# A projection tile moved into the index-score stage of a hybrid decoder block, with three PSUM pairs for the scores

## The reference, cut to what matters

```
h    = rmsnorm(x) * (1 + sc1) + sh1
proj = h @ w_in                      # cq, k, v, ki, wi, rq, rf, ri, rg, gates
qi   = rmsnorm(cq) @ w_uq_idx        # index queries, 8 heads of 64
q    = rmsnorm(cq) @ w_uq            # attention queries
score[t, s] = sum over heads of wi[t, head] * relu(qi[t, head] . ki[s])
f    = lb + (1 - lb) * sigmoid(rf)   # forget gate of the recurrence, head by head
qq   = silu(rq)                      # its query
```

## Time and profile before

| | |
|---|---|
| median of 3 runs | 1731.77 us (1730.85 to 1731.93) |
| the profiled execution | 1735.35 us |
| its span, first to last instruction | 1733.5 us |
| mean granted PE clock | 0.969 of full speed |
| PE busy | 1594.8 us, 92% |
| DVE busy | 1045.3 us, 60% |
| ACT busy | 713.5 us, 41% |
| POOL busy | 493.1 us, 28% |

### The profile page before, as it was taken

The page is one execution under the profiler, slowest core; times in us unless marked ns, Lnnn a source line. Parts: engine busy times, 40 slices in busy tenths (PEclk is TensorE's granted clock), DMA queues, the critical chain, the costliest instruction groups (busy, mean ns, idle before and its releaser), DMA issues.

```text
span 1733.5 us, 21047 instructions
## 1 busy us (share of the span) xinstructions
PE 1594.8 (92%) x7451; PEld 1252.6 (72%) x7451; DVE 1045.3 (60%) x1702; ACT 713.5 (41%) x1138; POOL 493.1 (28%) x371
## 2 busy tenths in 40 slices
PE   4897899999999997998999966999999999998996
PEld 3683477888888884445888755888888888887875
DVE  4677999835657486665456578555555555335345
ACT  5325523154656656565012434333333333222232
POOL 1410022243635442232000036455445543002001
PEclk8998999999999998999999978999999999999998
DMA  9562211221212212021434401222222323743441
GB/s 330 172 253 61 73 37 49 81 90 49 67 44 61 85 67 92 1 50 62 145 126 171 152 27 49 73 98 89 81 73 73 97 73 117 295 145 113 144 174 67
DMA packets 133931, 177.89 MB, mean 103 GB/s; under 512 B 9566, under 2 KB 91609, under 8 KB 133852
## 3 DMA queue, kind: packets, MB, share of 16 engines
q1 hardware_dynamic: 125210, 157.98, 27.9%
q10 hardware_dynamic: 8066, 16.78, 2.6%
q0 software_dynamic: 576, 2.10, 0.3%
HBM read 143.79 MB, written 32.52 MB: 102 GB/s over the span
## 4 chain that ended last, share of the span: by engine, by line
PE 81%; DVE 9%; ACT 3%; issue 3%; SPq 1%; POOL 1%; DMA 1%; DVEq 0%; ACTq 0%; POOLq 0%
PE pp L530 23%; PE pp L532 22%; PE pp L531 22%; PE pp L1670 3%; PE pp L1487 2%; DVE arena L2049 2%; PE pp L1493 2%; PE pp L1779 2%; PE pp L1809 2%; DVE cb_lo L2421 1%; DVE arena L2248 1%; SPq L648 1%; DVE h_part L2396 1%; DVE h_raw L2019 0%; DMA arena<-in_w_ada 0%
## 5 line engine op out<-in xcount | busy, mean ns | idle before, releaser
L530 PE MATMUL pp<-cb_hi,wp_hi 128*128 128x512 f32 x616 | 244.1, 396 | 29.3 <-DVE cb_lo L2421 16.0
L941 POOL TENSOR_TENSOR wp_sum<-raw 128x512 f32<-128x512 f32 x110 | 147.1, 1345 | 389.3 <-PE pp L532 386.8
L531 PE MATMUL pp<-cb_lo,wp_hi 128*128 128x512 f32 x616 | 243.1, 395 | 0.0
L532 PE MATMUL pp<-cb_hi,wp_lo 128*128 128x512 f32 x616 | 243.0, 394 | 0.0
L2405 DVE TENSOR_TENSOR wp_lo<-wp_sum,wp_hi 128x512 fp32r<-128x512 f32 x110 | 92.7, 845 | 161.4 <-ACT wp_hi L1378 161.4
L842 POOL TENSOR_TENSOR e_lo<-arena,e_hi 128x1024 fp32r<-128x1024 f32 (+1 forms) x38 | 96.0, 2528 | 294.2 <-ACT e_hi L1024 294.2
L530 PE MATMUL pp<-hT_hi,e_hi 128*128 128x512 f32 x416 | 168.3, 404 | 7.4 <-POOL hT_lo L834 6.0
L2071 DVE TENSOR_SCALAR_CACHE_REDUCE arena<-arena,bound 128x384 bf16<-128x384 f32 (+2 forms) x192 | 169.4, 941 | 0.8
L532 PE MATMUL pp<-hT_hi,e_lo 128*128 128x512 f32 x416 | 164.3, 395 | 0.0
L531 PE MATMUL pp<-hT_lo,e_hi 128*128 128x512 f32 x416 | 164.2, 395 | 0.0
L530 PEld LDWEIGHTS pp<-cb_hi,wp_hi 128*128 128x128 f32 x616 | 118.1, 192 | 55.8 <-issue 31.1
(11 more groups left out here) (258 smaller groups left out, 3258.7 us busy)
## 6 DMA issues: line engine op xcount, KB each, us to landing
arena<-in_w_ada SPq DMA_DIRECT2D x48, 512.0 KB, 8.0
raw<-in_w_ffn_down SPq DMA_DIRECT2D x44, 512.0 KB, 3.4
arena<-in_w_in SPq DMA_DIRECT2D x33, 512.0 KB, 3.7
raw<-in_w_ffn_gate SPq DMA_DIRECT2D x22, 512.0 KB, 5.0
raw<-in_w_ffn_up SPq DMA_DIRECT2D x22, 512.0 KB, 5.0
hidden_t<-stage SPq DMA_DIRECT2D x22, 512.0 KB, 3.1
hid_in<-hidden_t SPq DMA_DIRECT2D x44, 256.0 KB, 3.7
gates_t<-arena ACTq DMA_DIRECT2D x32, 256.0 KB, 2.1
```

What stands on the lines that cost most here:

```text
L530: nc.tensor.matmul(out, ah, bh, start=start and k == 0, stop=False)
L531: nc.tensor.matmul(out, ah, bl, start=False, stop=False)
L532: last = nc.tensor.matmul(out, al, bh, start=False, stop=stop and k == len(pairs) - 1)
L941: pool.tensor_tensor(wp_sum[n % 4], ff_weight(m, a), ff_weight(m, b), op).then_inc(sum_ready, 1)
```

## The change

The second head's forget tile `("rf", 1)` leaves its place between "ri" and `("rq", 1)`. It becomes sixteen steps of three products (one half, one block of channels), one behind each of the score pairs 6 to 21 (`fill_step`, `FILL_FROM = 6`). Its two halves accumulate in banks 0 and 1 meanwhile, so the scores keep `pp[1]` to `pp[3]`: item i uses `pp[1 + i % 3]`, and pair p waits for the first relu of pair p - 1 instead of for the second of pair p - 2. ACT takes the Sigmoid of the two halves after items 29 and 45.

The weights of `("rf", 1)` follow the index query weights in the ring, ahead of the attention query weights; SP issues them behind the last late modulation rows and the key copies. ACT rounds them before it copies the index queries, and takes the Sigmoid of `("rf", 0)` before that too. The first pair of scores no longer waits for that Sigmoid. The rounding of `("rq", 0)` moves from behind item 11 to behind item 19. The group numbers (`G_...`), which order the evictions, are renumbered. The diff, with parts that only rename left out:

```diff
     for name, done in (("uqi", (qi_full, 8)), ("uq", (pj_full, G_UQ + 8))):
         slot = len(ring.order) % 2
         ring.add(name, slot, ..., ring_uq[slot], done)
+        if name == "uqi":
+            plan_tile(("rf", 1), C_RF + P)
     plan_tile(("rq", 0), C_RQ)
     plan_rows("ri", [(C_RI, RW)])
-    plan_rf_rq(1)
+    plan_tile(("rq", 1), C_RQ + P)
...
# SP
-        load_from(("rf", 0), "uq")
+        load_from(("rf", 0), ("rf", 1))
         for n in range(24, 32):
             late_rows(n)
         sp.wait_ge(pj_free, G_B + 2)
         sp.dma_start(kT[0][HD:P, :], kT[0][0:HD, :]).then_inc(k_copied, 16)
         sp.dma_start(kT[1][0:HD, :], kT[1][HD:P, :]).then_inc(k_copied, 16)
-        load_from("uq", ("gate", 3, 3))
+        load_from(("rf", 1), ("gate", 3, 3))
# POOL
-        split_rests(("a", 0), ("rf", 0))
+        split_rests(("a", 0), ("rf", 1))
# ACT
+        act.wait_ge(cqt_full, 4)
+        for hf in range(2):
+            evac(G_RF0 + hf, sgT[0][:, hf * HALF:(hf + 1) * HALF], bank[hf], ACT.Sigmoid)
+        split_to(E[("rf", 1)])
         act.wait_ge(ada_summed, 25)
         for m in range(4):
             for hf in range(2):
                 act.wait_ge(qi_full, 2 * m + hf + 1)
                 act.activation(qiT[:, m, hf * HALF:(hf + 1) * HALF], bank[6 + hf], ACT.Copy).then_inc(qi_free, 1)
-        for hf in range(2):
-            evac(G_RF0 + hf, sgT[0][:, hf * HALF:(hf + 1) * HALF], bank[hf], ACT.Sigmoid)
...
-                act.activation(relu_buf[i % 2][:, 0:n], pp[i % 4][:, 0:n], ACT.Relu).then_inc(sc_relu, 1)
+                act.activation(relu_buf[i % 2][:, 0:n], pp[1 + i % 3][:, 0:n], ACT.Relu).then_inc(sc_relu, 1)
                 i += 1
-                if i == 12:
+                for hf in range(2):
+                    if i == 2 * (FILL_FROM + 8 * (hf + 1) + 1):
+                        evac(G_RF1 + hf, sgT[1][:, hf * HALF:(hf + 1) * HALF], bank[hf], ACT.Sigmoid)
+                if i == 20:
                     split_to(E[("rq", 0)])
...
# PE
+        def fill_step(hf, k):
+            e, g = E[("rf", 1)], G_RF1 + hf
+            if k == 0:
+                pe.wait_ge(e_lo_ready, e + 1)
+                pe.wait_ge(pj_free, g - 1)
+            cols = slice(hf * HALF, (hf + 1) * HALF)
+            last = split_product(bank[hf], [(e_hi[e % 2][:, k * P:(k + 1) * P], e_lo[e % 2][:, k * P:(k + 1) * P],
+                                             hT_hi[:, k, cols], hT_lo[:, k, cols])], k == 0, k == KD - 1)
+            if k == KD - 1:
+                last.then_inc(pj_full, 1)
+
         for p, (b, hp) in enumerate([(b, hp) for b in SCORED for hp in range(NIH // 2)]):
             n = P * (b + 1)
-            if p == 0:
-                pe.wait_ge(pj_free, G_RF0 + 2)
-            if p >= 2:
-                pe.wait_ge(sc_relu, 2 * p - 2)
+            if p >= 1:
+                pe.wait_ge(sc_relu, 2 * p - 1)
             for c0 in range(0, n, HALF):
                 c1 = min(n, c0 + HALF)
                 for e in range(2):
-                    last = pe.matmul(pp[(2 * p + e) % 4][:, c0:c1], ...)
+                    last = pe.matmul(pp[1 + (2 * p + e) % 3][:, c0:c1], ...)
...
+            if FILL_FROM <= p < FILL_FROM + 16:
+                fill_step(*divmod(p - FILL_FROM, KD))
-        pe.wait_ge(sc_relu, len(SCORED) * NIH - 3)
         for x in range(8):
             query_half(x)
...
         token_major(1, "ri", RW)
-        rfq(1)
-        pe.wait_ge(pj_free, G_RFQ[1] + 4)
+        one_tile(("rq", 1), G_RQ1)
+        pe.wait_ge(pj_free, G_RQ1 + 2)
```

More of the change, by code:

```diff
@@ L417, in build @@
     G_RF0 = G_B + 4
-    G_UQ = G_RF0 + 2
+    G_RF1 = G_RF0 + 2
+    G_UQ = G_RF1 + 2
     G_RQ0 = G_UQ + 8
[L420 to L423, removed]
+    G_RQ1 = G_RQ0 + 2
+    G_FIRST = G_RQ1 + 2
+    G_RFQ = [None, None, G_FIRST + 8, G_FIRST + 20]
+    RF_DONE = [G_RF0 + 2, G_RF1 + 2] + [g + 2 for g in G_RFQ[2:]]
+    RQ_DONE = [G_RQ0 + 2, G_RQ1 + 2] + [g + 4 for g in G_RFQ[2:]]
+    G_GATE = [G_FIRST] + [g + 4 for g in G_RFQ[2:]]
     G_GATE.append(G_GATE[2] + 8)
@@ L488, in build @@
         E_GROUP[("rf", h)], E_GROUP[("rq", h)] = RF_DONE[h] - 2, RQ_DONE[h] - 2
+    FILL_FROM = 6
     for q in range(4):
@@ L1144, in _ @@
             to_dram(G_UQ + x, ACT.Copy, qD[x // 2, :, (x % 2) * HALF:(x % 2 + 1) * HALF], over=spill_q)
[L1146 to L1151, removed]
         def logf(h):
@@ L1236, in _ @@
         logf(0)
-        split_to(E[("rf", 1)])
+        split_to(E[("rq", 1)])
         for t in range(NT):
@@ L1240, in _ @@
             act.activation(ri_tok[:, t, :], bank[t], ACT.Copy).then_inc(ks_read, 1)
-        rfq(1)
+        split_ahead(("rq", 1))
+        for hf in range(2):
+            evac(G_RQ1 + hf, rqT[1][:, hf * HALF:(hf + 1) * HALF], bank[hf], ACT.Silu)
         split_to(E[("gate", 0, 0)])
@@ L1586, in one_tile @@
                     pe.wait_ge(ks_read, g - G_RF0 + 1)
-                if g - G_RFQ[1] in (0, 1):
+                if g - G_RQ1 in (0, 1):
                     pe.wait_ge(ks_read, NT + 1 + g % 2)
@@ L1626, in _ @@
                 for e in range(2):
-                    last = pe.matmul(pp[(2 * p + e) % 4][:, c0:c1], qiT[HD * e:HD * (e + 1), hp, b * P:(b + 1) * P], kiT[HD * e:HD * (e + 1), c0:c1],
+                    last = pe.matmul(pp[1 + (2 * p + e) % 3][:, c0:c1], qiT[HD * e:HD * (e + 1), hp, b * P:(b + 1) * P], kiT[HD * e:HD * (e + 1), c0:c1],
                                      start=True, stop=True)
@@ L1630, in _ @@
                         last.then_inc(sc_full, 1)
-        pe.wait_ge(sc_relu, len(SCORED) * NIH - 3)
+            if FILL_FROM <= p < FILL_FROM + 16:
+                fill_step(*divmod(p - FILL_FROM, KD))
         for x in range(8):
             query_half(x)
-        def rfq(h):
-            one_tile(("rf", h), G_RFQ[h])
-            one_tile(("rq", h), G_RFQ[h] + 2)
         def half(x):
@@ L1715, in _ @@
         pe.wait_ge(mod_read, 5)
-        pe.wait_ge(pj_free, G_RFQ[1])
+        pe.wait_ge(pj_free, G_RQ0 + 2)
         pe.wait_ge(sc_relu, len(SCORED) * NIH)
         token_major(1, "ri", RW)
-        rfq(1)
-        pe.wait_ge(pj_free, G_RFQ[1] + 4)
+        one_tile(("rq", 1), G_RQ1)
+        pe.wait_ge(pj_free, G_RQ1 + 2)
         pe.wait_ge(ks_read, 2 * NT)
```

## The result

The changed kernel takes 1750.40 us (median of 4 runs, 1746.78 to 1752.46), the kernel before 1731.85 in the same comparison (4 runs, 1730.85 to 1735.25). The ratio is 1.0105, 95% interval 1.0087 to 1.0122: slower by 1%, as forecast, and 8.4 us above the 1742 that was predicted, 0.4 above the upper end of the range.

What follows compares the result with a forecast made beforehand. DVE was taken to pace the score stage and PE to bound what follows. Start +13.85, stage +7.3 and removal -10.9 sum to +10.2 us: 1745.6 profiled, median 1742, range 1734 to 1750, forecast given 62%.

Steps and rivals of the forecast that it cites:

- the term for the score stage: Score stage: with three pairs of banks, PE's pair and one relu stand in a row; 59.2 us instead of 51.9, +7.3.
- the rounding at item 20: Score stage, 640 columns: rounding the first query tile's weights there instead of at item 12 adds 0.4 us.
- The upper bound of the term, 11: Score stage: growth of 11 us with the low clock as far as pair 8 and no cover for the pieces.
- uncovered pieces: Score stage: two Sigmoid evictions, costed at nothing because PE's next pair covers them; 1.2 us without that cover.
- The start of the scores: Ahead of the first score: late forget weights, low clock in the query products, wait for query weights; +13.85 us together.
- the other case in the text, 3.3: Index query products after PE's idling: low clock loses 3.3 us, where the forecast took the dense case, 1.7.
- What was removed: Behind the scores: 48 products of the second forget tile leave PE, -10.9 us; 5.1 of DVE's 16.06 wait remains.
- The fill steps: Score stage: three products, 0.68 us, fit PE's gaps of 0.67 to 1.09; each tiling change costs 0.1; costed at nothing.
- the first rival: Score stage: drains or a lasting low clock push fill steps past their gaps; 5.4 more, +15.6, 1747.4 us; 18%.
- keep DVE's pace: Score stage: three pairs behave like four, so +7.3 goes; +2.9, 1734.7 us; 12%.
- The load was not there in time: Denies the rival that forget weights land before ACT's first copy, so its start hardly moves; -3.0, 1728.8 us; 8%.
- The sum: Whole kernel: +13.85 + 7.3 - 10.9 = +10.2 us on the profiled 1735.35, giving 1745.6.

Runs made afterwards that it cites:

- e2: Changed kernel with PE's wait for the attention query weights moved from ahead of the first score pair to behind the last; 1741.66 us, ratio 1.0058.
- e5: Changed kernel with the sixteen fill steps behind pairs 0 to 15 instead of 6 to 21; 1748.39 us, ratio 1.0095.
- e4: Kernel before with three pairs of banks for the scores instead of four, no fill steps and no load moved; 1755.33 us, ratio 1.0134.
- e1: Changed kernel with ACT's rounding of the second forget tile's weights behind the index query copies instead of ahead; 1736.27 us, ratio 1.0026.
- e6: Changed kernel with the second forget tile's weights loaded ahead of the late modulation rows and key copies; 1738.27 us, ratio 1.0026.
- e3: Changed kernel with ACT's rounding behind the index query copies and PE's query weight wait behind the scores; 1735.58 us, ratio 1.0028.
- e11: Kernel before with three pairs of banks and ACT's Sigmoid of the first forget tile ahead of the index query copies; 1750.57 us, ratio 1.0108.
- e8: Changed kernel with the forget weights loaded early, PE's query weight wait behind the scores, fill steps from pair 0; 1731.61 us, ratio 1.0001.
- e7: Kernel before, four pairs kept, with only ACT's Sigmoid of the first forget tile moved ahead of the query copies; 1729.23 us, ratio 0.9995.

## Why the prediction was right or wrong

**The failed step is the term for the score stage**, +7.3, which measured +12.63. Its mechanism, a pair and a relu in a row with two handoffs, holds to 0.02 us: pairs of 384 columns at half clock 2.23, of 768, 896 and 1024 at full clock 2.46, 2.77 and 3.09. Mis-sized was where the clock comes back. "The four pairs of 384 columns run at the low clock, as they do now" carries over from the kernel before a recovery that came there with PE busy 6.50 of 7.00 us. The three-pair order leaves PE half idle, so the old end of the low clock doesn't hold for it. By widths, measured against predicted: 384 columns 8.93 for 8.9; 512 columns 11.49 (168.42 to 179.91) for 7.2; 640 columns 9.91 for 8.9; 768 and 896 together 20.93 for 20.8; the rest 13.24 for 13.4. Of the +4.3 at 512 columns 4.0 is the low clock in pairs 4 to 7, for which e2 at full clock takes 7.52, and 0.3 the two steps that don't fit. That the clock is the cause is shown by e2 (no idling: stage 57.65), e5 (dense: back in 5.4 us) and e4 (sparse, low for fourteen pairs: 70.05). The further +1.0, at 640 columns, is in the main the rounding at item 20; this is read from the trace, and no run moves that rounding. GpSimd's subtraction that follows it, kernel after:

```profile
185.78 2.51 POOL L849 TENSOR_TENSOR e_lo<-arena,e_hi 128x1024 fp32r<-128x1024 f32 x1 [15.60 <-ACT e_hi L1031]
```

It ran beside DVE's addition, which took 2.62 for 0.89, and ACT's next relu waited 2.14 for it. The prediction let that subtraction slow DVE nowhere in the stage, although the kernel before shows it: beside the same subtraction (156.91 to 159.26) an addition took 2.46 us (from 157.35) where its neighbours took 0.76.

The upper bound of the term, 11, was too low by its own wording as well: the low clock on the four pairs of 512 columns costs 4 x (2.08 - 1.13) = 3.8, and with the 1.2 of uncovered pieces the 7.3 becomes 12.3.

**The start of the scores** was right in every step: landing 8.66 (8.6 taken), the first copy 12.4 later against PE's first product, the query weights 3.68 (3.7). Only the low clock in the six products lost 2.65 and not 1.7: 13.15 for 10.5. That is the second small size, 0.95 of the 1.06 by which the term was off; the other case in the text, 3.3, was nearer.

**What was removed** gave 10.12 of 10.9 at equal low-clock time, and DVE's wait fell to 3.10, near the 5.1 worked out.

**The fill steps** cost what was taken. At full clock 0.89 us lie between a step's first product and the next pair's (170.68 to 171.57 in e5), 0.68 and two changes of 0.1. From 768 columns on pairs come as they do without steps; at 512 and 640 columns 0.15 and 0.05 stick out. The Trainium skill (TensorEngine Tiling (Array Packing), Tiling Modes) has a change of mode drain the engine; nothing here speaks against that, but both changes of a step together cost 0.21 us, so the 5.4 of the first rival was not the drains. Its other half, "a clock that stays low", is what came, from the pairs without a step; its time, 1747.4, was the nearest of those forecast, but by luck: its 5.4 was worked out for drains in pairs 6 to 21.

**The other rivals.** The score stage didn't keep DVE's pace: ACT waited for PE, not for DVE, at all widths but 640. The load was not there in time. e1 and e6 show what that rival was worth, 12 to 14 us less; but with its other terms as they came out the kernel was still slower by 0.26%, since the stage at low clock outweighed the removal.

**The median.** The sum stood against the profiled execution, 1745.6 against 1751.36 measured. Of the 5.8 missing, 5.3 is the stage, 1.1 the start, 0.8 the removal, and -1.4 the early part, which differs from run to run. The last 2.6 to the median came from carrying over the 3.6 by which the profiled execution of before lay above its median; that of after lay 1.0 above.

## What to carry to other kernels

A stretch at the low clock in a profile belongs to the order that made it: before carrying its length over, ask what kept PE busy at its end, and whether the change leaves that there. A wait of a few us ahead of a half-idle stage can cost more by the low clock behind it than by its own length: 6.85 us against 2.95 in the kernel after (e2). Put the wait where its data is needed, which gave 8.7 us here (e2); making the stage's first us dense shortened the low stretch to 5.4 us, but gave little by itself (e5). Work that fills gaps belongs first into the gaps next to such a wait, and then where it fits without sticking out.

## What the runs showed of the hardware that was not expected

In a half-idle stage the granted clock mostly stayed at the level that it had. Pairs of 0.92 us with gaps of 0.57 to 0.69 left it at 2.4 GHz (e2). Pairs of the same length went to 1.2 GHz just behind one gap of 1.57 (e3) or 1.86 (e11). There pairs of 1.65 to 2.93 us with gaps of 0.57 to 0.89 left it low for 37 us (e11) and 41 us (e4), and then it rose with the gaps no shorter. Dense work got it back in 5.4 us (e5). The length of a gap is not all of it: one of 2.08, with a step behind each pair, left the clock at 1.00 (e8), and one of 2.19 brought it down for 3.4 us (e7). What tips the clock, down or up, no run here settles.

Single DVE operations beside a subtraction on GpSimd were longer: 2.62 us for 0.89 (the addition at 640 columns in the kernel after), 1.87 for 0.42 (the first multiplication in e3). The Trainium skill (GPSIMD Engine Reference, 1. Specifications) names contention over SBUF with DVE instructions that have two SBUF inputs; the addition is such a one and agrees. The multiplication, one tile by a column of weights, was longer too; no run here tells whether it is in the two-port mode that the page also names.
